# Expert inputs gathered by row from memory, expert results combined by TensorE inside the loop, in a two-layer decoder with a mixture of experts

## The reference

```python
x = x + mixer(rmsnorm(x, norm_mix[l]))              # convolution, or attention
h = rmsnorm(x, norm_ffn[l])
# router: the best of 4 groups, in it the best 2 of 8 experts, each with a weight w
for each token, for each of its 2 experts e:
    x += w * (silu(h @ w_gate[e]) * (h @ w_up[e])) @ w_down[e]
```

## Time and profile before

| | us |
|---|---|
| Median of 3 runs | 1690.32 (1688.18 to 1690.77) |
| Profiled execution, its time | 1688.36 |
| Profiled execution, its span | 1686.6 |
| TensorE busy in the span | 1564.3 (93%) |
| VectorE, ScalarE, GpSimd busy | 587.2, 387.5, 86.2 |
| Gate and up products L816, 2080 | 462.3 |
| Down products L840, 1040 | 237.5 |
| Gathering products L784, 552 | 230.0 |
| Mean granted TensorE clock | 0.968 |

### The profile page before, as it was taken

One profiled execution on the slowest core, in us unless ns is written; L12 is line 12 of the kernel. 1 busy time (PEld: TensorE's weight loads), 2 busy tenths in 40 slices (PEclk: granted clock), 3 DMA queues, 4 the chain that ended last, 5 costly groups with the idle time before them and its releaser, 6 DMA issues. The chain is left out here.

```text
span 1686.6 us, 18294 instructions
## 1 busy us (share of the span) xinstructions
PE 1564.3 (93%) x6924; PEld 737.3 (44%) x6924; DVE 587.2 (35%) x1587; ACT 387.5 (23%) x790; POOL 86.2 (5%) x93
## 2 busy tenths in 40 slices
PE   8999988999999999949999999996999999999992
PEld 4444444444444443325554455554444444444340
DVE  2111255222222221255264587545322222222225
ACT  2000131111111111132243478522111111111112
POOL 0000010000000000000000000011000000000000
PEclk9999998999999999979999899997999999999996
DMA  6261218999999999964310300035999999999994
GB/s 200 75 275 49 67 74 349 425 426 425 425 426 426 425 426 426 418 197 131 100 51 1 150 2 1 17 150 198 396 426 426 425 426 426 425 426 426 426 403 169
DMA packets 110101, 469.48 MB, mean 278 GB/s; under 512 B 26416, under 2 KB 53040, under 8 KB 59312
## 3 DMA queue, kind: packets, MB, share of 16 engines
q1 hardware_dynamic: 104800, 459.75, 66.9%
q0 software_dynamic: 5200, 8.40, 1.3%
HBM read 457.63 MB, written 19.14 MB: 283 GB/s over the span
## 5 line engine op out<-in xcount | busy, mean ns | idle before, releaser
L816 PE MATMUL ps<-raw,e_xT 128*64 128x512 f32 x2080 | 462.3, 593 | 22.4 <-DMA raw<-in_expert_w_up 21.7
L816 PEld LDWEIGHTS ps<-raw,e_xT 128*64 128x64 f32 x2080 | 152.1, 137 | 320.7 <-issue 319.3
L917 DVE TENSOR_TENSOR e_sg_hid<-e_sg_hid,ps 64x512 f32<-64x512 f32 x65 | 44.3, 681 | 567.0 <-ACT e_sg_hid L863 567.0
L840 PE MATMUL ps<-raw,e_hT 128*64 128x512 f32 x1040 | 237.5, 598 | 0.0
L406 PE MATMUL ps<-c_hT,raw 128*128 128x512 f32 x384 | 165.0, 592 | 0.2 <-ACT c_hT L351 0.2
L868 ACT ACTIVATE e_ysb<-ps 64x512 f32<-64x512 f32 x130 | 77.0, 592 | 289.3 <-PE ps L840 288.5
L863 ACT ACTIVATE e_sg_hid<-ps 64x512 f32<-64x512 f32 x65 | 38.6, 593 | 399.0 <-PE ps L816 399.0
L784 PE MATMUL ps<-m_xhi,e_pick 128*128 128x512 f32 x276 | 118.9, 431 | 9.3 <-DVE e_pick L886 9.3
L840 PEld LDWEIGHTS ps<-raw,e_hT 128*64 128x64 f32 x1040 | 68.9, 136 | 122.3 <-issue 111.4
L1467 PE MATMUL ps<-a_spare,raw 128*128 128x512 f32 x256 | 113.8, 601 | 1.5 <-ACT a_spare L1174 1.5
L406 PEld LDWEIGHTS ps<-c_hT,raw 128*128 128x128 f32 x384 | 72.9, 190 | 91.7 <-issue 91.1
(11 more groups left out here) (226 smaller groups left out, 1390.1 us busy)
## 6 DMA issues: line engine op xcount, KB each, us to landing
raw<-in_expert_w_gate SPq DMA_DIRECT2D x130, 1024.0 KB, 23.6
raw<-in_expert_w_up SPq DMA_DIRECT2D x130, 1024.0 KB, 24.7
raw<-in_expert_w_down SPq DMA_DIRECT2D x130, 1024.0 KB, 24.5
raw<-in_conv_w_in SPq DMA_DIRECT2D x12, 1024.0 KB, 9.6
k_rows<-pairs_y SPq DMA_DIRECT2D x6, 1024.0 KB, 9.8
raw<-in_w_kv SPq DMA_DIRECT2D x6, 1024.0 KB, 7.2
raw<-in_conv_w_out SPq DMA_DIRECT2D x1, 4096.0 KB, 18.2
raw<-in_attn_w_in SPq DMA_DIRECT2D x4, 1024.0 KB, 5.5
```

Source lines behind the costliest of these rows:

```text
L816: mm = pe.matmul(ps_gu[C - C * i:2 * C - C * i, :], xT[:, q % 2, k, u * C:(u + 1) * C], ring(m, L, p)[:, kk * F:(kk + 1) * F], start=(k == ...
L840: mm = pe.matmul(ps_y[c % 2][n * C:(n + 1) * C, :], hT[:, 2 * h + kk, :], ring(m, L, p)[:, kk * D + n * 512:kk * D + (n + 1) * 512], start ...
L917: dve.tensor_tensor(hid, sg, ps_gu[0:C, :], ALU.mult).then_inc(s_hid, 1)
```

## The change

- **Rows in memory.** The normed rows are stored contiguously by k (`by_k_out`: VectorE reads x with a stride of 8 elements), and `sync_ring` copies each tile to `rows_x` in memory, 0.5 MB each, the last one behind the prefetch of pieces 8 to 11. High and low parts of x are gone. Before issuing pieces 12 to 15, SyncE waits for the four copies.
- **Table.** `table` on VectorE turns each pair's place into a column (chunk) and a row (place in the chunk), codes both as 0/1 arrays, and TensorE's product of them (`tensor_table`, 8 products) gives the token of each place. From it come the indices `idx` and, later, `pick`. A second table, with weights, is formed in chunk 0 (16 products).
- **Gathering by GpSimd.** An indirect DMA fetches 128 rows (two chunks) by index into `rows`. The first two are issued before the router's block ends; in the loop one is issued in every second step, for the group two ahead. `pe_gather`, its eviction L857, `dve_pick` with 8 operations per group and `dve_dest` are gone.
- **Combining in the loop.** The result of a chunk stays in SBUF, weighted, as high part (ScalarE) and low part (VectorE), with columns 0 to 511 on partitions 0 to 63 and columns 512 to 1023 on 64 to 127. In the two steps of the next group, between gate and up products and transposes, TensorE multiplies `pick` by both parts, 8 products of 64 places for each of the 4 token tiles, into two pairs of PSUM banks, and VectorE adds each tile to x in two halves. Overflow chunks combine themselves, four tiles each. The last pair (30, 31) is combined after the loop.
- **After the loop.** The norm that follows is in the same block, per tile behind its last addition. In the first layer the block then ends, semaphores are cleared, and `shared_kv` starts with all 32 transposes (their input now contiguous); its first weights are loaded during the norm. Scatter, read-back, `Combine` and `final_norm` are gone. `vector_normed` reads x with a stride too, in the convolution's norm as well.
- **VectorE's order.** `vector_tail` now precedes the moves of the first transposed rows.

```diff
     def sync_ring(self, sp):
-        sp.wait_ge(self.s_o, 2 * NT)
-        prefetch(sp, self.m, self.L, range(8, 12))
+        for t in range(NT):
+            if t == NT - 1:
+                sp.wait_ge(self.s_o, 2 * NT)
+                prefetch(sp, self.m, self.L, range(8, 12))
+            sp.wait_ge(self.s_xn, t + 1)
+            sp.dma_start(self.m.rows_x[self.L][t * P:(t + 1) * P, :], self.xn[:, t, :]).then_inc(self.s_out, 16)
...
+    def first_rows(self, pool):
+        pool.wait_ge(self.s_o, 1)
+        pool.memset(self.rows[:], 0.0).then_inc(self.s_zero, 1)
+        pool.wait_ge(self.s_zero, 1)
+        pool.wait_ge(self.s_idx, 2)
+        pool.wait_ge(self.s_out, 16 * NT)
+        for q in range(2):
+            self.gather(pool, q)
...
+        def table():
+            slot = m.slot[:].rearrange("p t k -> p (t k)")
+            col, row = self.pos[:, 0], self.pos[:, 1]
+            own.step(dve.tensor_scalar(col, slot, 0.5 - C / 2, MAGIC * C, ALU.add, ALU.add))
+            own.step(dve.tensor_scalar(col, col, MAGIC * C, None, ALU.subtract))
+            own.step(dve.tensor_tensor(row, slot, col, ALU.subtract))
+            dve.tensor_tensor(self.chot[:], self.col[:].unsqueeze(1).broadcast_to([P, NTK, NCH]),
+                              col.unsqueeze(2).broadcast_to([P, NTK, NCH]), ALU.is_equal).then_inc(self.s_own, 1)
...
+            own.step(dve.tensor_tensor(self.rhot[:], m.iota[:, 0:C].unsqueeze(1).broadcast_to([P, NTK, C]),
+                                       row.unsqueeze(2).broadcast_to([P, NTK, C]), ALU.is_equal))
+            dve.tensor_tensor(self.ctok[:], self.chot[:], m.token[:].rearrange("p t k -> p (t k)").unsqueeze(2)
+                              .broadcast_to([P, NTK, NCH]), ALU.mult).then_inc(self.s_hot, 1)
...
+            dve.wait_ge(self.s_tok, 1)
+            own.step(dve.tensor_scalar(far, found, 0.5, FAR, ALU.is_lt, ALU.mult))
+            for u in range(PAIR):
+                dve.scalar_tensor_tensor(out=self.idx[u * C:(u + 1) * C, :], in0=found[:, u::PAIR], scalar=-1.0,
+                                         in1=far[:, u::PAIR], op0=ALU.add, op1=ALU.add).then_inc(self.s_idx, 1)
...
         def pe_turn(pe, n):
             q, h = n // 2, n % 2
+            pe.wait_ge(r.s_rows[q % 2], 16 * (q // 2 + 1))
+            wait(pe, s_xev, n)
...
+        def pe_combine(pe, chunks, t, banks, done):
+            for c in chunks:
+                pe.wait_ge(s_pick, c + 1)
+                pe.wait_ge(s_ylo, c + 1)
+            for c in chunks:
+                for part in (yhi, ylo):
+                    for n in range(2):
+                        half, last = slice(n * C, (n + 1) * C), c == chunks[-1] and part is ylo
+                        mm = pe.matmul(banks[n][:], pick[half, pick_place(c), t * P:(t + 1) * P],
+                                       part[half, y_place(c), :], start=(c == chunks[0] and part is yhi), stop=last)
+                        if last:
+                            mm.then_inc(done, 1)
...
         def pe_step(pe, c):
             pe_gate_up(pe, c)
-            pe_gather(pe, c + PAIR)
+            q = c // PAIR - 1
+            if PAIR <= c < E:
+                for t in (2 * (c % 2), 2 * (c % 2) + 1):
+                    pe_tile(pe, (PAIR * q, PAIR * q + 1), t, 4 * q + t)
...
             pe_transpose(pe, c)
-            pe_turn(pe, c + PAIR)
+            if c + PAIR < NCH:
+                pe_turn(pe, c + PAIR)
             pe_down(pe, c)
...
+        def dve_step(dve, c):
+            if 0 < c < E:
+                dve_low(dve, c - 1)
             wait(dve, s_sg, c + 1)
             wait(dve, s_ht, c)
             dve.tensor_tensor(hid, sg, ps_gu[0:C, :], ALU.mult).then_inc(s_hid, 1)
...
+            if PAIR <= c < E:
+                dve_add(dve, t, 4 * q + t)
             wait(dve, s_ht, c + 1)
             wait(dve, s_used, c * NPIECE)
             dve.tensor_copy(hT[:].rearrange("p k c -> p (k c)"), ps_h[:, 0:KF * C]).then_inc(s_hev, 1)
+            if c + PAIR < NCH:
+                dve_turned(dve, c + PAIR)
+            if PAIR <= c < E:
+                dve_add(dve, t + 1, 4 * q + t + 1)
+            if c < E and c % PAIR:
+                for i in (c - 1, c):
+                    dve_pick(dve, i)
```

More of the change, by code:

```diff
@@ L57 @@
 HK = NK // 2
+NCH = E + N_OVF
+NTK = 2 * NT
 class Chain:
@@ L566, in tensor, with tensor_table @@
         mm.then_inc(self.s_rank, 1)
+        pe.wait_ge(self.s_hot, 1)
+        self.tensor_table(pe, m.ps[4], self.rhot[:], self.ctok[:], 1).then_inc(self.s_tok, 1)
+    def tensor_table(self, pe, bank, rows, cols, halves):
+        for i in range(NTK):
+            for u in range(halves):
+                mm = pe.matmul(bank[u * C:(u + 1) * C, 0:NCH], rows[:, i, :], cols[:, i, :],
+                               start=(i == 0), stop=(i == NTK - 1))
+        return mm
     def scalar(self, act):
@@ L718, in vector @@
         slots()
+        table()
     def vector_tail(self, dve):
@@ L893, in dve_dest @@
[L893 to L903 removed]
+            if c == 0:
+                act.wait_ge(s_wtab, 1)
@@ L973, in _ @@
         @block.gpsimd
         def _(pool):
-            n = chunks(pool, lambda c: pool_step(pool, c))
-            for half in s_st:
-                pool.wait_ge(half, E // 2 * 16)
-            with pool.If(0 < n):
-                pool.wait_ge(s_st[0], (n + (E + 1) >> 1) * 16)
-                pool.wait_ge(s_st[1], (n + E >> 1) * 16)
-            pool.nop().then_inc(s_landed, 1)
+            for c in range(E):
+                pool_step(pool, c)
+            overflow(pool, lambda c: pool_step(pool, c))
@@ L994, in _ @@
+            overflow(dve, lambda c: dve_step(dve, c))
+            for t in range(NT):
+                last_add(t, 0)
+                if t:
+                    nrm.vector_mean(dve, t - 1)
+                last_add(t, 1)
+                if t:
+                    nrm.vector_root(dve, t - 1)
+                    scaled(t - 1)
+            nrm.vector_mean(dve, NT - 1)
+            nrm.vector_root(dve, NT - 1)
+            scaled(NT - 1)
         @block.tensor
@@ L1165, in _ @@
         def _(act):
-            act.activation(m.rstd[:, 4, 0:1], m.part[:], ACT.Sqrt)
-            for t in range(NT):
-                act.wait_ge(arrived.added, t + 1)
-                nrm.scalar_tile(act, t, xn[:, t, :])
             act.wait_ge(s_gain, 32)
```

434 lines of the change are left out of this document (206 added, 228 removed).

## The result

The changed kernel takes 1704.35 us (median; 1702.92 to 1706.15) against 1689.25 us of the kernel before on the same chip: ratio 1.009, 95% interval 1.0072 to 1.0107. It is 0.9% slower; the prediction was 1686.8 us with a range up to 1697. The profiled execution has a span of 1700.7 us, against 1686.6.

A forecast was written before the change was run, and what follows sets the result against it. The stream of expert weights was taken to bound the loops, TensorE having 0.38 us per chunk in hand. First layer +0.3, second layer -4.6 and start +0.8 gave -3.5 us, so 1686.8 against a median of 1690.3; range 1678 to 1697.

The forecast's parts named there:

- The loop on TensorE: Expert loops: 2.24 us per chunk removed, 2.1 added for sixteen combining products; chunk 13.8 to 14.1, still under 14.34.
- TensorE becomes the bound: Rival, expert loops: sixteen combining products per chunk take 2.6 us or more and set the time, mostly 1690 to 1705; chance 0.17.
- Stream and loop end: Weight stream in each layer's expert loop: starts 4.2 us later, closes a hole, ends +2.4 per layer (+1 to +5).
- Router tail: Before each layer's expert loop: the experts' block starts 4.2 us later (+3 to +7), at 263.3 in the first layer.
- two gathers by POOL: End of the router's block: two gathers hold GpSimd 1.1 us each, +2.2 (1.8 to 3.6).
- contention with GpSimd gone: Router tail: without GpSimd's subtraction the VectorE operation beside it falls from 2.70 to 0.24 us, -2.46.
- strided normed: Router tail: VectorE reads normed rows at a stride of 8 elements, 1.5 us against 1.28, +0.3 (0 to 1.2).
- Start: First norm before the first mixer: the copy is strided too, +0.8 us on the last tile.
- End of the first layer: Last down product to first feature product: 28.3 us instead of 30.4, -2.1; with the loop's +2.4, +0.3.
- End of the second layer: Last down product to the span's end: 27.1 us instead of 33.5, -6.4; with -0.6 and the loop's +2.4, -4.6.
- Start eats the end: Rival, router tails and block change: gathers hold GpSimd 1.8 us each, block change takes 2.0; no change, 1690.2; chance 0.22.

The follow-up runs named there:

- e7: Changed kernel with constants reordered and 192 unused bytes, so all 16 ring slots begin at multiples of 512 bytes; 1694.5 us, 1.0023 to before.
- e3: Changed kernel with scaled copies of the first norm and the norm behind the first layer's loop contiguous again, transposes strided; 1700.64 us, 1.0055 to before.
- e4: Changed kernel with code for 2 overflow chunks instead of 16, same work done; 1698.3 us, 1.0047 to before.
- e11: Changed kernel with the ten later slots padded to a multiple of 512 bytes, 128 more bytes behind them, first six unmoved; 1693.2 us, 1.002 to before.
- e12: Changed kernel with the first early gather in the router's block, the second at the start of the experts' block; 1704.05 us, 1.0086 to before.
- e16: Changed kernel with weight pieces 8 to 11 issued only when the indices are ready, just ahead of the two early gathers; 1719.39 us.
- e2: Changed kernel without the gathers inside the loops, first two pairs' rows reused (doesn't compute the reference); 1682.28 us, 0.9958 to before.
- e8: Changed kernel, both early gathers moved to the experts' block, three of four weight pieces meant to wait for them; 1706.57 us, 1.0098 to before.
- e17: Changed kernel, all slots at multiples of 512, norm copies and router's normed rows contiguous, second early gather after the block change; 1687.2 us, 0.9987 to before.

## Why the prediction was wrong

The time was predicted at -3.5 us and came out at +14.1 in the spans, 17.6 us off: the loops account for 10.1, the router's tails for 9.3, the start for 1.1, the second layer's end for 2.2; the first layer's end and the attention stage go the other way, by 2.7 and 2.3.

- *The loop on TensorE*: right. 2.1 us were predicted for sixteen products, 1.96 measured; chunk 13.8 predicted, 13.6 measured; waits for weights fill the later part of the second layer's loop, from 1357 on and so more than the last third. The rival that TensorE becomes the bound did not happen, the weight loads stay hidden at 0.235 us per pair (each takes 0.18 to 0.19 us in the loop, where the prediction quotes 0.107), and VectorE's copy of hT did not delay the down products.
- *Stream and loop end*: **failed**. The step took 425 GB/s for granted ("the DMA share at 1.0 from the first piece") and counted bytes only. Counted at an equal rate it held: in e7 first piece to last down product is 465.4 and 480.1, 2.0 and 3.8 us under before, against 1.8 and 2.4 predicted. What is in its place is the ring's start, moved from 84480 to 85824 by a larger iota and other constants: +5.5 and +6.2 us (after against e7). No row of the trace of before shows what a slot's start is worth; that the change moves the slots could be worked out from the tensor sizes in the two kernels.
- *Router tail*: **one step failed**, "two gathers by POOL", sized 1.1 us each by what they hold GpSimd. They do (1.16 and 1.00). The sentence "The block can't end before both are issued; the first lands about as the next block starts" is the wrong one: the block can't end before both have landed. From the indices (262.9) to the block's first piece it takes 6.8 us: 0.95 until the first gather starts, 1.5 to the start of the second, 4.1 to its landing, 0.3 to the block. The kernel before took 0.48 from its slots to that piece: +6.4, 2.2 predicted. The other terms: contention with GpSimd gone, as said; strided normed +0.77 (+0.3 taken from the earlier trace rows, bound 1.2); table 4.13 (4.2).
- *Start*: +1.9, not +0.8. The copy's 0.4 falls on all four tiles, not on the last alone (e3: -1.45 when undone).
- *End of the first layer*: -4.8, -2.1 predicted. Copies 1.15 (1.5 taken), 32 transposes 5.1 in all, where 5.0 was set for 24; change of blocks 1.4 as taken; against this VectorE's jump, 1.7.
- *End of the second layer*: -4.2, -6.4 predicted. The missing step is the jump over the unused overflow code, 3.8 us on the path, 3.3 of them won back in e4.
- *Attention*, -2.3: no cause shown. The kernels run here whose attention code is that of the changed kernel lie between 395.8 and 399.2 in this stage, with the 398.1 of the kernel before among them.
- *Start eats the end* had the right place, the gathers in the router's tail, and asked for the wrong quantity: not what holds GpSimd, but what the block waits for.

With the ring back at a multiple of 512 the change is still 0.2% slower than before (e11, e7), which is about what can be told from no change; with the other edits it is 0.25% faster.

## What to carry to other kernels

When a change adds or resizes any tensor, look at where the large DMA targets begin afterwards, and pad them back to a multiple of 512 bytes: here that was worth 10 us, three times what the whole change was forecast to win. A gather that GpSimd issues at the end of a block is priced by its landing, not by its instruction; issuing it in the next block helps only if it then doesn't queue behind the stream that it is to start. Work that a long wait used to cover (a jump over unused code, a change of blocks) becomes bare when the wait goes.

## What the runs showed of the hardware

- Pieces of 1 MB to 128 partitions, back to back at a DMA share of 1.01, into a ring of 16 slots: 426 GB/s with the ten later slots at multiples of 512 bytes, 420 to 421 with these 128, 320, 384 or 448 bytes beyond one. The six first slots 128 beyond: nothing measured; 320 beyond: about 3 us in two loops, at the edge of what can be told.
- A block in which GpSimd issued gathers opens the next one 0.3 to 0.4 us after their last landing (269.7, 267.8 and 276.2 us in the changed kernel, e12 and e16); it does not wait for a piece of weights that SyncE issued in it (landing at 277.1, e16).
- A gather for 128 places (rows of 4 KB) issued with no stream beside it lands 3.6 to 4.4 us after its issue (changed kernel, e2, e12); the median of all, most of them beside the stream, is 8.2, it took 10.6 behind four pieces just issued (e16), and one costs the stream 0.75 us.
- A `nop` behind GpSimd's gathers counted its semaphore before the second gather had started (SyncE went on at 265.05, the gather stands at 266.19 us, e8).
- Going on behind the code of 16 unused chunks took VectorE 3.07 us (two: at most 1.34, a wait for a product), behind that of 15 it took TensorE 3.8 (one: 0.7), changed kernel against e4.
- VectorE reading at a stride of 8 elements and writing contiguously: 2.05 us instead of 1.28 (two inputs, 1024 elements; e17), 1.15 instead of 0.75 (one input; e3).
- Two products of 64 rows x 512 columns in the two halves of the array: 0.235 us per pair, with their weight loads of 0.18 to 0.19 us each hidden.
